# Every second multiplication of the sandwich norm moves from VectorE to GpSimd in two gaps of a fp32 diffusion backbone

## What is computed

```python
x = x + gt1 * rms_norm(y_lat, norm_g[l, 1])            # end of one sub-layer
h = modulate(rms_norm(x, norm_g[l, 2]), sh2, sc2)      # start of the next
x = x + gt2 * rms_norm(swiglu(h, ...), norm_g[l, 3])
```

## Time and profile before

| | |
|---|---|
| median of 3 runs | 1262.39 us (1262.36 to 1262.87) |
| the profiled execution | 1263.51 us |
| its span, first to last instruction | 1261.8 us |
| busy: PE, DVE, ACT, POOL | 94%, 50%, 45%, 10% |
| mean granted TensorE clock | 0.974 of full speed |

### The profile page before, as it was taken

How to read it: one execution, slowest core, us unless ns; L and a number is a source line. 1 busy time by engine, 2 the same in 40 slices (tenths; PEclk the granted TensorE clock), 3 DMA queues, 4 the chain that set the end, 5 groups by cost and what they waited for, 6 DMA issues and landing times.

```text
span 1261.8 us, 17880 instructions
## 1 busy us (share of the span) xinstructions
PE 1182.8 (94%) x7085; PEld 923.8 (73%) x7085; DVE 625.2 (50%) x1002; ACT 568.7 (45%) x1071; POOL 120.6 (10%) x116
## 2 busy tenths in 40 slices
PE   6899989989899999999999899999989997999996
PEld 3577734558378888888888558788779875888885
DVE  2532268652543332333222375589976525666554
ACT  2622246753462222223222376775355435665552
POOL 0030320110001111011000000010024100111000
PEclk9899999999999999999999999999979998999998
DMA  9655556642553333333333463234003042666560
GB/s 344 208 163 150 168 197 218 207 114 84 159 141 100 101 100 91 93 96 92 93 99 106 138 150 80 66 89 117 18 20 85 22 131 81 179 189 185 173 178 34
DMA packets 239390, 159.54 MB, mean 126 GB/s; under 512 B 14778, under 2 KB 213836, under 8 KB 239308
## 3 DMA queue, kind: packets, MB, share of 16 engines
q1 hardware_dynamic: 238528, 158.11, 42.5%
q10 hardware_dynamic: 780, 0.29, 0.1%
HBM read 157.33 MB, written 1.05 MB: 126 GB/s over the span
## 4 chain that ended last, share of the span: by engine, by line
PE 81%; DVE 9%; ACT 6%; issue 2%; DMA 1%; SPq 1%; POOL 0%; DVEq 0%; ACTq 0%; POOLq 0%
PE bank L1382 43%; PE bank L1393 9%; PE bank L1394 4%; PE bank L1369 2%; PE bank L1486 2%; PE bank L1436 2%; PE bank L1591 2%; PE bank L1467 1%; PE bank L1601 1%; DVE blocks L1020 1%; DVE outer L1018 1%; ACT h_work L1723 1%; PE bank L778 1%; PE bank L1622 1%; DMA w_raw<-in_ada_w 1%
## 5 line engine op out<-in xcount | busy, mean ns | idle before, releaser
L1382 PE MATMUL bank<-h_both,w_hi 128*128 128x512 f32 x1296 | 404.9, 394 | 2.5 <-issue 2.5
L1918 DVE TENSOR_TENSOR w_lo<-w_raw,w_hi 128x1024 fp32r<-128x1024 f32 (+1 forms) x179 | 220.5, 1234 | 244.3 <-ACT w_hi L1690 243.9
L1382 PEld LDWEIGHTS bank<-h_both,w_hi 128*128 128x128 f32 x1296 | 242.8, 188 | 53.7 <-issue 3.5
L1382 PE MATMUL bank<-h_both,w_lo 128*128 128x512 f32 x648 | 253.1, 391 | 0.0
L1690 ACT ACTIVATE w_hi<-w_raw 128x1024 fp32r<-128x1024 f32 (+1 forms) x179 | 184.0, 1031 | 72.5 <-PE bank L1382 52.9
L1382 PEld LDWEIGHTS bank<-h_both,w_lo 128*128 128x128 f32 x648 | 122.1, 188 | 25.9
L1393 PE MATMUL bank<-h_both,w_hi 128*128 128x512 f32 x308 | 113.0, 405 | 6.2 <-DVE h_both L1971 3.2
L1382 PE MATMUL bank<-act_both,w_hi 128*128 128x512 f32 x352 | 108.4, 389 | 0.0
L2176 POOL TENSOR_TENSOR act_both<-a_tmp,act_both 128x512 fp32r<-128x512 f32 (+1 forms) x44 | 44.7, 1016 | 466.1 <-ACT act_both L1792 283.9
L1394 PE MATMUL bank<-h_both,w_lo 128*128 128x256 f32 x308 | 87.5, 284 | 0.0
L1382 PEld LDWEIGHTS bank<-act_both,w_hi 128*128 128x128 f32 x352 | 66.1, 188 | 13.8
(11 more groups left out here) (283 smaller groups left out, 1693.0 us busy)
## 6 DMA issues: line engine op xcount, KB each, us to landing
w_raw<-in_ada_w SPq DMA_DIRECT2D x96, 512.0 KB, 5.0
w_raw<-in_ffn_w_gate_up SPq DMA_DIRECT2D x88, 512.0 KB, 3.8
w_raw<-in_ffn_w_down SPq DMA_DIRECT2D x32, 512.0 KB, 3.8
w_raw<-in_gdn_w_in SPq DMA_DIRECT2D x32, 512.0 KB, 4.0
w_raw<-in_attn_w_in SPq DMA_DIRECT2D x14, 512.0 KB, 3.9
w_raw<-in_ffn_w_down SPq DMA_DIRECT2D x16, 384.0 KB, 3.4
w_raw<-in_gdn_w_out SPq DMA_DIRECT2D x8, 512.0 KB, 5.2
w_raw<-in_attn_w_in SPq DMA_DIRECT2D x8, 256.0 KB, 3.5
```

The lines of the kernel that those rows point to most:

```text
L1382: m = nc.tensor.matmul(dst, stationary(a, k), moving(b, k), start=(first and k == kk[0] and a == b == 0), stop=(last and k == kk[-1] and a ...
L1918: nc.vector.tensor_tensor(w_lo[where[key] % N_RAW][:, 0:tiles, 0:w], raw_slot(key)[:, 0:tiles, 0:w], w_hi[m % N_SPLIT][:, 0:tiles, 0:w].bi ...
```

## The change

In gaps 0 and 1, POOL multiplies the tiles 1, 3, 5 and 7 of `y` by `post_rstd`, and DVE the tiles 0, 2, 4 and 6. All additions stay on DVE. A new semaphore, `pool_scaled`, tells DVE of each tile from POOL. The norms at 256 tokens (i = 2 and 3) are as before.

```diff
+        pool_scaled = sem("pool_scaled")
...
                 for k in range(KT + 1):
-                    if k < KT:
+                    pooled = i < 2
+                    if k < KT and not (pooled and k % 2):
                         nc.vector.tensor_tensor(y_views[i][:, k, lo:T], y_views[i][:, k, lo:T],
                                                 post_views[i][0][:, lo:T], ALU.mult).then_inc(post_scaled, 1)
+                    if k and pooled and k % 2 == 0:
+                        dve.wait_ge(pool_scaled, (i * KT + k) // 2)
+                    elif k:
+                        dve.wait_ge(post_scaled, (i * KT + k + 1) // 2 if pooled else (i - 2) * KT + KT + k)
                     if k:
-                        dve.wait_ge(post_scaled, i * KT + k)
                         nc.vector.tensor_tensor(xT[:, k - 1, lo:T], y_views[i][:, k - 1, lo:T], xT[:, k - 1, lo:T],
                                                 ALU.add).then_inc(x_updated, 1)
...
+            def post_norm(i):
+
+                wait_evacuated(pool, ("post", i))
+                for k in range(1, KT, 2):
+                    nc.gpsimd.tensor_tensor(y_views[i][:, k, :], y_views[i][:, k, :], post_views[i][0],
+                                            ALU.mult).then_inc(pool_scaled, 1)
...
+            post_norm(0)
             ffn(0)
+            post_norm(1)
             if LAST_SUB == 3:
                 gdn_gpsimd(pool, link)
```

## The result

| | before | changed |
|---|---|---|
| median | 1262.39 us (1261.07 to 1262.87, 5 runs) | 1267.99 us (1267.51 to 1269.27, 5 runs) |
| span of the profiled execution | 1261.8 us | 1265.8 us |
| mean granted clock in it | 0.974 | 0.972 |

The changed kernel is slower: ratio 1.0047, 95% interval 1.0032 to 1.0062, or +5.6 us by the medians. That lies inside the stated range (1265.1 to 1268.4) and 1.7 us above the forecast of 1266.3.

A forecast was written before the change was run, and what follows sets the result against it. DVE's multiplications and additions were taken to bound the gaps, blocked in turn by POOL: 2 x 1.95 = +3.9 us on the median 1262.39 gave 1266.3 us, range 1265.1 to 1268.4.

The forecast's parts named there:

- the clock's case: Rival, 10%: PE's clock falls in a longer gap and slows the last three sums, up to 2.7 us; 1267.6 to 1269.
- What bounds the kernel: In gap 0 the chain runs through DVE's 16 instructions; a microsecond more or less there moves the kernel's end by one.
- those shares are the gaps: Whole kernel: the 9% DVE and 6% ACT of the chain that ended last were taken to be the gaps.
- DVE's part of a gap: First multiplication to last addition's end: 11.7 us against 9.72, about 1.95 us longer in each of gaps 0 and 1.
- its lower bound of 1.8: Low end for DVE's loss in a gap: a POOL turn of 1.11 us gives 1.8 us per gap.
- The order of the turns: In each gap DVE goes first, then DVE and POOL alternate while POOL has work: 4 x (0.55 + 1.15) = 6.8 us.
- the rival of another order: Rival, 10%: DVE or POOL keeps the port; a gap takes 12.2 to 12.3 us, +2.6 per gap, 1267.6 us.
- The exchange 0.14 us before the end: At each DVE/POOL exchange in a gap, the waiting engine begins its work 0.14 us before the other ends.
- the rival of the wholly blocked instruction: Rival, 4%: each instruction blocks the other engine until finished; exchanges 7.9 us, a gap 12.8 us, 1268.6 in all.
- Engines side by side: Rival, 5%: DVE and POOL do not block each other in the gaps; some 3 us faster, 1259.4.
- It ends some 1.5 us behind the last square, as before: PE's sums at a gap's end, 0.89 us per tile, were to finish as far behind the last square as before.
- No cost elsewhere: Outside gaps 0 and 1: POOL's next work 20 us away isn't moved; norms at 256 tokens costed at nothing.

The follow-up runs named there:

- e3: Kernel before, with eight POOL memsets of an unused 128x512 tile added per gap, so that POOL only writes: 1261.9 us against 1262.63, ratio 0.9993.
- the filler: Unused fp32 products of 128x512 on PE, two ahead of the first sum of squares and two behind it per gap, added to the changed kernel: 1266.9 us.
- e5: Changed kernel with odd tiles added last, and DVE reading the norm factor from PSUM and putting its products there: 1261.45 us against 1262.49, ratio 0.9993.
- e4: The changed kernel with the filler in gaps 0 and 1: 1266.9 us against 1262.63, ratio 1.0033.
- e6: Kernel of e5 with two unused products on PE ahead of the first sum of squares in each gap: 1258.36 us against 1262.49, ratio 0.9969.
- e8: Control: kernel before with only two unused products on PE ahead of the first sum of squares in each gap: 1261.79 us against 1262.59, ratio 0.9998.
- e11: Kernel of e6 unchanged, timed once more against the kernel before: 1258.95 us against 1262.82, ratio 0.9972.

## Why the prediction was right, and where it wasn't

The mechanism on DVE was right, and the sum fell 1.7 us short because of PE. That the median lies in the range all the same is owed to the width given for other orders and for a part of the clock's case, not to the sum.

- **What bounds the kernel**: right for gap 0. But "those shares are the gaps" was not: of the chain's 9% on DVE, 113 us, some 67 lie in the delta rule (800 to 960 us) and 12 around gap 0. It changed nothing, as the sum went by the rows of the gaps.
- **DVE's part of a gap** was forecast at 11.7 us, with an alternation of turns of 0.55 and 1.15 us, from the stretched `w_lo` in the FFN. It took 11.59. Two stretched DVE instructions start 1.68 us apart, for 1.70 forecast. The gap's loss on DVE is 1.87 us in place of 1.95, between the forecast and its lower bound of 1.8. Right.
- **The order of the turns**: DVE first, then strictly in turn. Right, and with it the rival of another order (12.2 to 12.3 us) falls. One of the two grounds for it was none: the earlier trace rows has a copy held up by a memset, where e3 has memsets that hold up no multiplication or addition. It is another conflict than this one.
- **The exchange 0.14 us before the end**: the rival of the wholly blocked instruction would have given 12.8 us per gap, and it was 11.59. Where the Trainium skill has the lock held for the whole instruction ("SBUF — State Buffer", "SBUF: two separate sides"), a DVE turn and a POOL turn here take 1.68 us together, not 0.69 + 1.27 = 1.96: the next instruction begins some 0.14 us before the recorded end of the last one.
- **Engines side by side**: fell in both directions. In the changed kernel DVE's instructions take 1.63 to 1.75 us beside POOL in place of 0.68, and POOL's 1.71 in place of 1.27.
- **"It ends some 1.5 us behind the last square, as before"** is the step that failed. PE ended 2.71 and 2.37 us behind it, at half clock. I had the clock as a rival, 10%, up to 2.7 us in one of the gaps; it came in both. The loss of 5.7 us is 3.7 of block, for 3.9 forecast, and 2.0 behind it that the sum put at nothing. Of these the filler gave back 1.7 (1.0 in gap 0, 0.7 in gap 1), the clock's part. The other 0.25 us, in gap 1, stay at full clock: even there PE now ends 1.70 us behind the last square and not 1.44. The rows did hold the warning: half speed in gap 1 in the kernel before. I argued that it cost nothing there, which was so, and did not ask what a longer idle stretch in front of the same sums would do.
- **No cost elsewhere**: right; with gap 0 alone changed, gap 1 kept 13.25 us.

## What to carry to other kernels

Before work goes from VectorE to GpSimd, look at where the operands of what stays on VectorE lie. If its instructions read two SBUF tensors, those beside a reading GpSimd instruction wait for it in turn, so the shift pays only if GpSimd's turn is shorter than the VectorE work it takes away (here it was not: (11.59 - 9.72) / 4 + 0.60 = 1.07 against 0.60 us); with one of the two inputs in PSUM the engines ran side by side here. And a wait of TensorE that is a little longer can cost more than its length, if the products that follow it set the end.

## What the runs showed that I had not expected

- A POOL product with the same tensor on both inputs held DVE up for 0.84 us, one of two tensors for about 1.07 (1.75 - 0.68). Whether it is the equal operand or the chain of semaphores between those products was not tried.
- The same kernel (e5) had PE at full clock through both gaps in one execution and at 0.87 of it in another. What decides between them is open. The length of the idle stretch alone does not: in the kernel before, PE is idle for 2.30 us ahead of the sums in both gaps, and the clock falls in gap 1 only. Two unused products in each idle stretch kept the clock at 1.00 in the gaps in all four profiles with them (e4, e6, e8, e11). Whether they also narrow the spread of the times is not shown: it was 4.9 us over 12 executions of e5, 3.2 over 6 of e6 and 2.9 over 7 of e11, but fewer executions spread less by themselves.
- ACT can do Ln and Exp in place in a PSUM bank and DVE take the factor from there at 0.69 us per 128x512, no slower than from SBUF.
